# Block 3's chunked scan: the level loop of the triangular inverse written out, with the transposes and the A·V products dealt out inside it

## The reference

```python
def step(state, inp):
    r_t, w_t, k_t, v_t, kk_t, a_t = inp
    removed = jnp.einsum('bhvk,bhk->bhv', state, kk_t)
    state = (state * w_t[:, :, None, :]
             - removed[..., None] * (kk_t * a_t)[:, :, None, :]
             + v_t[..., None] * k_t[:, :, None, :])
    return state, jnp.einsum('bhvk,bhk->bhv', state, r_t)
```

## Time and profile before

| | before |
|---|---|
| median of 3 runs | 3749.22 us (3747.87 to 3749.76) |
| profiled execution, own time | 3749.22 us |
| span of its profile | 3747.4 us |
| TensorE matmul busy | 3420.9 us (91%) |
| VectorE, ScalarE, GpSimd busy | 2090.2, 1755.2, 1048.0 us |
| `rwkv_scan` in the trace | from 3130.1 us to some 3266 us |
| the levels' loop | 3152.8 to 3186.0 us |

### The profile page before, as it was taken

How to read it: one execution, slowest core, us unless ns; L and a number is a source line. 1 busy time by engine, 2 the same in 40 slices (tenths; PEclk the granted TensorE clock), 3 DMA queues, 4 the chain that set the end, 5 groups by cost and what they waited for, 6 DMA issues and landing times. The chain is left out here.

```text
span 3747.4 us, 55692 instructions
## 1 busy us (share of the span) xinstructions
PE 3420.9 (91%) x20889; PEld 2767.9 (74%) x20889; DVE 2090.2 (56%) x2469; ACT 1755.2 (47%) x2293; POOL 1048.0 (28%) x435
## 2 busy tenths in 40 slices
PE   6989999969999999999999697899998976779997
PEld 4877777648888888888888483678887855668876
DVE  3320121259999999999999326421241154346665
ACT  3222333237777777777777424322233242133333
POOL 1334222202323232232323130134443300024443
PEclk9999999979999999999999798799999877889999
DMA  8223443249999999999999427022222200012321
GB/s 271 83 67 97 123 127 117 82 140 365 368 381 364 384 362 378 375 371 378 364 383 365 159 91 282 23 90 90 96 96 68 80 29 4 6 57 90 101 90 40
DMA packets 245420, 696.64 MB, mean 186 GB/s; under 512 B 17846, under 2 KB 149802, under 8 KB 186652
## 3 DMA queue, kind: packets, MB, share of 16 engines
q1 hardware_dynamic: 234956, 657.73, 47.3%
q0 software_dynamic: 9936, 36.18, 3.7%
q10 hardware_dynamic: 384, 0.65, 0.0%
HBM read 668.73 MB, written 30.23 MB: 187 GB/s over the span
## 5 line engine op out<-in xcount | busy, mean ns | idle before, releaser
L315 POOL TENSOR_TENSOR split_w<-ring,split_w 128x1024 fp32r<-128x1024 f32 (+1 forms) x294 | 696.4, 2369 | 1712.0 <-ACT split_w L310 1563.5
L1831 DVE TENSOR_TENSOR moe_low<-ring,moe_high 128x2048 fp32r<-128x2048 f32 x408 | 929.3, 2285 | 23.4 <-ACT moe_high L1822 23.3
L1822 ACT ACTIVATE moe_high<-ring 128x1024 fp32r<-128x1024 f32 x810 | 827.7, 1058 | 103.5 <-PE psum L2074 102.1
L310 ACT ACTIVATE split_w<-ring 128x1024 fp32r<-128x1024 f32 (+1 forms) x294 | 304.8, 1037 | 1036.8 <-PE psum L380 650.7
L2070 PE MATMUL psum<-moe_high,moe_xe 128*128 128x512 f32 x2176 | 586.8, 392 | 0.0
L2070 PEld LDWEIGHTS psum<-moe_high,moe_xe 128*128 128x128 f32 x2176 | 410.4, 189 | 85.1
L1982 POOL DMA_INDIRECT moe_y_rows<-moe_ye,moe_target x34 | 197.4, 5807 | 695.7 <-DVE moe_ye L1886 695.7
L380 PE MATMUL psum<-pair,split_w 128*128 128x512 f32 x1584 | 363.4, 392 | 12.0 <-PEq L128 5.2
L380 PEld LDWEIGHTS psum<-pair,split_w 128*128 128x128 f32 x1584 | 299.7, 189 | 75.0 <-issue 8.1
L380 PE MATMUL psum<-b_pair,split_w 128*128 128x512 f32 x1440 | 338.4, 397 | 14.5 <-PEq L848 8.8
L2074 PE MATMUL psum<-moe_low,moe_xe 128*128 128x512 f32 x1088 | 337.3, 391 | 0.0
(11 more groups left out here) (590 smaller groups left out, 4302.6 us busy)
## 6 DMA issues: line engine op xcount, KB each, us to landing
ring<-in_w_experts SPq DMA_DIRECT2D x408, 1024.0 KB, 7.2
ring<-in_w_mod SPq DMA_DIRECT2D x48, 1024.0 KB, 6.4
ring<-in_w_in SPq DMA_DIRECT2D x39, 1024.0 KB, 5.3
ring<-in_w_up SPq DMA_DIRECT2D x33, 1024.0 KB, 5.1
ring<-in_w_in SPq DMA_DIRECT2D x44, 512.0 KB, 5.2
ring<-in_w_down SPq DMA_DIRECT2D x20, 1024.0 KB, 5.0
ring<-in_w_gate SPq DMA_DIRECT2D x11, 1024.0 KB, 5.3
ring<-in_w_out SPq DMA_DIRECT2D x8, 1024.0 KB, 5.3
```

Of the source, the lines that this page charges most:

```text
L310: self.nc.scalar.activation(high, raw, ACT.Copy).then_inc(self.K.rounded, 1)
L315: self.nc.gpsimd.tensor_tensor(low, raw, high.bitcast(F32), ALU.subtract).then_inc(self.K.split, 1)
L1822: self.nc.scalar.activation(self.B["high"][:, j % HALVES, :], self.raw(j), ACT.Copy).then_inc(self.high, 1)
L1831: self.nc.vector.tensor_tensor(flat("low"), self.K.ring[:, self.ring_slot(j // 2), :], flat("high").bitcast(F32), ALU.subtract).then_inc(s ...
```

## The change

The hardware loop over the levels becomes a Python loop, so that its instructions are written out four times. `both(4, kappa)` is moved to stand right behind `both(0, beta)`. The sixteen fills leave their two places and are dealt out, two behind each half's off·T matmuls; ScalarE's takes are dealt out in the same way behind its copies to X. `ka_read` is waited for ahead of the first fill in place of ahead of the loop. The semaphore `joining` and its increments go. The count on `turned` is kept as one for the first transpose in place of two, and the waits on it follow.

```diff
                 both(0, beta).then_inc(ba_done, 1)
+                both(4, kappa).then_inc(ka_done, 1)
...
-                for f in range(3 * NT):
-                    fill(f)
-                pe.wait_ge(taken, 3 * NT)
-                both(4, kappa).then_inc(ka_done, 1)
-                pe.wait_ge(ba_read, 1)
-                pe.wait_ge(ka_read, 1)
-                with pe.Fori(0, L) as l:
+                for l in range(L):
                     for m in range(2):
-                        pe.wait_ge(off_ready, 2 * l + (m + 1))
-                        pe.wait_ge(turned, 2 * l + (m + 1))
-                        pe.sem_inc(joining, 1)
+                        pe.wait_ge(off_ready, 2 * l + m + 1)
+                        pe.wait_ge(turned, 2 * l + m if l else 1)
+                        if l == 0 and m == 0:
+                            pe.wait_ge(ba_read, 1)
                         for b in range(16):
                             for cc in range(CT):
                                 ins = nc.tensor.matmul(ps[rows(cc), m, b * C:(b + 1) * C], off[rows(cc), 16 * m + b, :],
                                                        T[rows(cc), 16 * m + b, :], start=True, stop=True)
                         ins.then_inc(xd, 1)
+                        if l == 0 and m == 0:
+                            pe.wait_ge(ka_read, 1)
+                        for f in range(2):
+                            fill(4 * l + 2 * m + f)
                     for m in range(2):
-                        pe.wait_ge(x_ready, 2 * l + (m + 1))
-                        pe.sem_inc(joining, 1)
+                        pe.wait_ge(x_ready, 2 * l + m + 1)
...
-                for f in range(3 * NT, 4 * NT):
-                    fill(f)
...
-                for f in range(3 * NT):
-                    take(f)
                 for l in range(L):
                     for m in range(2):
                         sc.wait_ge(xd, 2 * l + m + 1)
                         nc.scalar.activation(X[:, 16 * m:16 * m + 16, :], by(m, 1, C), ACT.Copy).then_inc(x_ready, 1)
-                for f in range(3 * NT, 4 * NT):
-                    take(f)
+                        for f in range(2):
+                            take(4 * l + 2 * m + f)
...
-                nc.vector.transpose(T.rearrange("p b n -> p (b n)"), TT.rearrange("p b n -> p (b n)")).then_inc(turned, 2)
+                nc.vector.transpose(T.rearrange("p b n -> p (b n)"), TT.rearrange("p b n -> p (b n)")).then_inc(turned, 1)
```

More of the change, by code:

```diff
@@ L3471, in rwkv_scan @@
         n_(s) for s in "fill taken u at un corr rt g gready chain state y yready".split())
-    loads0, joining = K.loads_n, n_("joining")
+    loads0 = K.loads_n
     H, L, C, W = RW_H, len(LEVELS), RWKV_C, CT
```

## The result

The changed kernel takes 3769.53 us (median of 4 runs, 3765.54 to 3773.89) against 3748.55 us (4 runs, 3747.57 to 3749.76): a ratio of 1.0051, with a 95% interval of 1.0039 to 1.0063. By the medians that is slower by 21.0 us, by the ratio 19.1 (14.6 to 23.6), where 24.1 were forecast. The profiled execution has a span of 3767.3 us against 3747.4, +19.9 us.

The account below looks back on a forecast made before the run. TensorE's fresh small-matmul code was taken to be bound by the arrival of its pieces. Terms 21.7 + 1.0 + 1.3 + 0.1 = +24.1 us on 3749.2 gave 3773 us, range 3762 to 3784 (0.79).

Parts of the forecast that it names:

- (a): In the unrolled levels, transposes of the dealt-out fills delay the next code piece: +1.0 us, bounds 0 to 7.6.
- (b): In the solve after the levels, TensorE starts at half clock instead of full: +1.3 us, bounds 0 to 7.4.
- the shift: Behind the solve's first matmul the code is the same, so the whole +24.1 us delay lasts to the end.
- the arrival of code bounds the stretch: In the scan, TensorE's fresh small-matmul code is paced by arriving 128-record pieces, 3.72 us each, not matmuls, copies or semaphores.
- 21 pieces at 3.72 us: From the 3134.31 boundary to the solve, 21 pieces put the last boundary at 3212.4 instead of 3190.68: +21.7 us.
- The 9.5 us of earlier start: Moving both(4, kappa) ahead of the fills starts the levels' first matmuls 9.5 us earlier, already inside the +21.7 us.
- (c): Last wait before the solve is for VectorE's subtraction (0.68 us) in place of ScalarE's take (0.60): +0.1 us.
- The first: Rival: straight code arrives in time in the levels and the overlap pays, -12.8 us, 3736 us; chance 0.07.
- The second: Rival: code arrival partly hidden, 2.6 to 3.0 us a piece, -2 to +7 us, 3747 to 3756; chance 0.05.
- The third: Rival: waits in the levels add to the pieces, slower still, +39 us, 3788; chance 0.09 beyond 3784.

## Why the prediction was right

The forecast of 3773 us (3762 to 3784) had the cause and the way right; it was 3 to 5 us too high (+24.1 against +21.0 by the medians and +19.1 by the ratio), which the points on (a), (b) and the shift account for.

- **That the arrival of code bounds the stretch.** Right. Writing out the loop alone costs 31.1 us of solve start, 7 us of added work cost 2.0, the instruction queue moved 13 transfers more, and bodies short enough to be held lose their gaps.
- **21 pieces at 3.72 us.** Right. From 3133.17 to 3212.03 stand 21 pieces in 78.86 us, 3.76 each. The boundary ahead of the solve came 82.5 us behind the scan's start in place of 60.5 (3190.68 - 3130.14); +22.0 against +21.7 forecast. Part of that closeness is luck: the 21 pieces took 0.7 us more than forecast, and the scan's first boundary came 0.5 us sooner than in the old trace (3.65 against 4.17 us).
- **The 9.5 us of earlier start.** Measured 10.0 (22.6 - 12.7), and worth 9.1 in the comparison with the loop written out alone. It was real, and less than a third of what the copies take.
- **(a), the fills' delay, +1.0.** Small, as taken. The 21 pieces hold whatever delay there was, and took 78.86 us against 21 x 3.72 = 78.1: 0.7 us at most, unless other pieces were quicker than the mean. The doubled transposes show 0.6 us for another set, within the noise; the upper end of 7.6 was far off.
- **(b), the clock in the solve, +1.3.** Right about the line, wrong about what it costs. The solve took 9.42 us (3213.43 to 3222.85) against 7.65, +1.8, and the clock returned inside it (mean 0.74). But a longer solve also gives the piece behind it time to arrive: the gap in line 3583 is 0.51 us at 3224.66, where it was 1.76 at 3202.70. From the last boundary ahead of the solve to that gap, three pieces in both kernels, it is 12.63 us against 12.02. So (b) and (c) together were worth 0.6 us, where +1.4 were taken; the prediction added TensorE's work in a stretch that the arrival of code paces. In the levels the mean was 0.67, not the 0.50 that I expected, since the transposes and A·V fills made some parts dense; it made little difference to the pieces.
- **(c), +0.1.** From the last boundary to the solve 1.40 us in place of 1.32.
- **"The shift goes through to the end."** Partly wrong. Measured from the scan's first matmul, the shift is +22.0 us at the boundary ahead of the solve, +22.6 at the gap of 3224.66 and +22.0 at VectorE's last copy of the scan (3287.15 against 3265.75); +22.7 was forecast for the first, with (a), and +24.1 for the others. Yet the span grew by only 19.9. Of the other 2.1 us, 0.6 is that the new trace entered the scan 0.6 us earlier, and 1.5 are behind the scan. Both are well within what the ten traces differ by ahead of the scan, 8.9 us, so they are chance, as far as these runs show. The stretch from line 3583 to the chain's last steps took 63.1 us in place of 64.9: 1.25 us of that is the shorter first gap, the rest goes with a clock of 0.81 in place of 0.79 (the last row of windows above, and the one of the kernel before below). I gave later clock changes no term, only a sentence.

```profile
3199.65:3264.50 64.85, 46.84 (x2005) 41.74 (x2003) 13.82 (x23) 1.68 (x3) 0.00 (x0) 0.79 0.02 4
```

- **The rivals.** The first (straight code arrives in time) would have shown levels of 5.8 us; none had that without a held copy. The second needs 2.6 to 3.0 us a piece, and they took 3.76. The third (39 us) would have needed 7.6 us from (a) and 7.4 from (b), where some 0.7 and 0.6 were measured.
- What the Trainium skill, "Runtime: NRT & Kernel Launch", section "Instruction fetch mechanics", says of a block's boundary ("mostly hidden") and its preference for full unrolling don't hold for code of this kind: a piece of 32x32 float32 matmuls is executed in 1.3 to 2 us and takes 3.7 to arrive.

## What to carry to other kernels

Count the instructions of small matmuls, not only their time: where the trace has gaps released by "issue" at equal numbers of instructions, with as many transfers on the instruction queue, the engine's code is what arrives late, as it was here, and a loop that runs from a held copy can be worth more than the overlap that writing it out allows (here 31.1 us against 9.1). Here the break-even was plain to work out beforehand: copies added, times the length of a gap-to-gap stretch, against the waits removed. To use the idle time of such stretches, put work in them that is long for its code (128x128 transposes), and keep the loop.

## What the runs showed of the hardware

- A fresh piece of TensorE's code, 128 records of matmul with weight load, 16 KB, mostly took 3.3 to 4.3 us to the next wherever its own work was shorter, at either clock level. The next piece is asked for only when the one before is under way: of the piece that starts at 3156.43 in the earlier trace rows, 1.35 us pass until the transfer of the next begins, it runs from 3157.78 to 3158.71, and 1.4 us more pass until the engine goes on at 3160.14, 3.71 us in all. A wait at the head of a piece isn't used: the piece at 3149.49 ran 17 records, then waited until 3152.76, its successor's transfer began only at 3153.73, and the piece lasted 6.94 us.
- Loop bodies of 4 and 6 pieces were held from pass to pass, one of 8 wasn't, and one of 7 was fresh again only in the third of four passes. I had not expected the alternation: a body one piece too long lost 5.30 us at its third turn and all its pieces, then ran clean again in the fourth.
- The first turn of the hardware loop into a held body cost 0.15 to 0.20 us of TensorE's time; the later turns lie under waits of some 0.45 us on VectorE.
